# Two transformer blocks on one core: a tenth k-pair per half of the down projections by seven products, with the stationary sums in a ring of nine places

## The reference, cut to what matters

```
x = x + (gelu(u_gate) * u_val) @ w_ffn_down        # block 1: [256, 5632] @ [5632, 2048]
x = x + (silu(gate) * up) @ w_ffn_down_2           # block 2: the same shapes
```

## Time and profile before

| | us |
|---|---|
| median of three runs | 2571.33 |
| the profiled execution, its own time | 2572.12 |
| its span, from the first to the last instruction | 2570.2 |
| PE busy (share of the span) | 2559.9 (100%) |
| DVE busy | 1693.3 (66%) |
| ACT busy | 1346.9 (52%) |
| SP, raw weights of the down projections: 88 loads of 1024 KB | 4.9 each from issue to landing (median) |

### The profile page before, as it was taken

One profiled execution on the slowest core, in us unless ns is written; L12 is line 12 of the kernel. 1 busy time (PEld: TensorE's weight loads), 2 busy tenths in 40 slices (PEclk: granted clock), 3 DMA queues, 4 the chain that ended last, 5 costly groups with the idle time before them and its releaser, 6 DMA issues.

```text
span 2570.2 us, 34530 instructions
## 1 busy us (share of the span) xinstructions
PE 2559.9 (100%) x12410; PEld 2131.0 (83%) x12410; DVE 1693.3 (66%) x2069; ACT 1346.9 (52%) x1729; POOL 99.6 (4%) x110
## 2 busy tenths in 40 slices
PE   9999999999999999999999999999999999999998
PEld 8887788888888888888887888888888888888887
DVE  6656556877777788875667565465555554547888
ACT  5455545666555554555645466434544444445454
POOL 2000000111111100000000000000000000000000
PEclk9999999999999999999999999999999999999999
DMA  7745555666665575655555545555566665657564
GB/s 242 220 149 156 165 188 172 215 206 206 189 188 190 167 284 196 225 184 187 186 172 156 164 154 158 194 190 183 177 209 198 215 197 187 193 186 255 203 216 161
DMA packets 281419, 493.82 MB, mean 192 GB/s; under 512 B 14578, under 2 KB 123236, under 8 KB 281056
## 3 DMA queue, kind: packets, MB, share of 16 engines
q1 hardware_dynamic: 277952, 478.73, 57.3%
q0 software_dynamic: 3184, 13.41, 1.6%
q10 hardware_dynamic: 176, 0.27, 0.1%
HBM read 483.17 MB, written 9.18 MB: 192 GB/s over the span
## 4 chain that ended last, share of the span: by engine, by line
PE 98%; DVE 1%; ACT 0%; issue 0%; DVEq 0%; ACTq 0%
PE acc L771 19%; PE acc L773 19%; PE acc L772 19%; PE acc L1071 13%; PE acc L1064 7%; PE tp L1115 3%; PE tp L1117 3%; PE tp L1116 3%; PE acc L1115 3%; PE acc L1117 3%; PE acc L1116 3%; PE tp L799 1%; PE tp L862 1%; PE tp L844 1%; PE tp L854 0%; PE tp L908 0%
## 5 line engine op out<-in xcount | busy, mean ns | idle before, releaser
L1941 DVE TENSOR_TENSOR WL<-WR,WH 128x1024 fp32r<-128x1024 f32 x712 | 882.7, 1241 | 704.6 <-ACT WH L1392 703.4
L1392 ACT ACTIVATE WH<-WR 128x1024 fp32r<-128x1024 f32 x712 | 754.0, 1059 | 878.1 <-PE acc L773 717.3
L771 PE MATMUL acc<-WH,A 128*128 128x512 f32 x1328 | 523.7, 394 | 0.4 <-DVE A L2009 0.3
L773 PE MATMUL acc<-WH,A 128*128 128x512 f32 x1328 | 517.5, 390 | 0.0
L772 PE MATMUL acc<-WL,A 128*128 128x512 f32 x1328 | 517.1, 389 | 0.0
L1071 PE MATMUL acc<-A,WH 128*128 128x512 f32 x1408 | 336.4, 391 | 0.0
L1071 PEld LDWEIGHTS acc<-A,WH 128*128 128x128 f32 x1408 | 258.6, 188 | 50.0
L771 PEld LDWEIGHTS acc<-WH,A 128*128 128x128 f32 x1328 | 249.4, 188 | 54.1 <-issue 4.0
L773 PEld LDWEIGHTS acc<-WH,A 128*128 128x128 f32 x1328 | 249.3, 188 | 53.0
L772 PEld LDWEIGHTS acc<-WL,A 128*128 128x128 f32 x1328 | 249.6, 188 | 49.7
L771 PE MATMUL acc<-WH,XH 128*128 128x512 f32 x544 | 216.4, 398 | 0.0
(11 more groups left out here) (387 smaller groups left out, 3100.5 us busy)
## 6 DMA issues: line engine op xcount, KB each, us to landing
WR<-in_w_in_dram SPq DMA_DIRECT2D x199, 512.0 KB, 3.6
WR<-in_w_ffn_up_dram SPq DMA_DIRECT2D x176, 512.0 KB, 3.6
RAW<-in_w_ffn_down_dram SPq DMA_DIRECT2D x88, 1024.0 KB, 4.9
WR<-in_w_ffn_in_dram SPq DMA_DIRECT2D x176, 512.0 KB, 3.4
WR<-in_w_out_dram SPq DMA_DIRECT2D x64, 512.0 KB, 3.5
WR<-in_w_in_dram SPq DMA_DIRECT2D x65, 256.0 KB, 3.0
WR<-in_w_ple_gate_dram SPq DMA_DIRECT2D x32, 512.0 KB, 4.3
WR<-in_w_branch_a_dram SPq DMA_DIRECT2D x16, 512.0 KB, 3.7
```

Of the source, the lines that this page charges most:

```text
L771: pe.matmul(o, H[:, kt + k, cols], WH[:, s, k], start=begin, stop=False)
L773: mm = pe.matmul(o, L[:, kt + k, cols], WH[:, s, k], start=False, stop=end)
L1392: act.activation(WH[:, n % RING], WR[:, n % RING], ACT.Copy).then_inc(hi_done, 1)
L1941: dve.tensor_tensor(WL[:, n % RING], WR[:, n % RING], WH[:, n % RING].bitcast(F32), ALU.subtract).then_inc(lo_done, 1)
```

## The change

It makes ten instead of nine k-pairs of each half sevens, with new strings for the order, and keeps `STA` at nine places: place k modulo 9 for the k-th seven of a stage (of which there are now 20). The first nine loads stand at steps 2 to 10 of the stage, as before; each further one stands behind the raw weights of the step that is seven steps ahead of its seven, and SP waits for `q_used` of the seven that had the place before. In halves 1 and 3, where the sums of the first half were used again before, the sums are loaded anew. Four semaphores are taken in turn for the loads, so SP also waits there for the load four before. PE now waits for the sums at every seven. During the up projections a tenth set of sums is made and stored.

```diff
-SUM_J = 9
+SUM_J, STA_SLOTS = 10, 9
 PER_HALF = FKT // 2
-EARLY, LATE = "8878787878787878787888", "8887878787878787878788"
+EARLY, LATE = "8878787877878778787888", "8887878787787877878788"
...
-SUM_GROUPS = (range(0, 1), range(1, 2), range(2, 5), range(5, SUM_J))
+SUM_SEMS = 4
+SEVENS = [[q for q in stage if q.seven] for stage in (QUADS1, QUADS2)]
...
-        STA = sb("STA", [P, SUM_J, 2, 3 * P], F32R, at=stationary)
+        STA = sb("STA", [P, STA_SLOTS, 2, 3 * P], F32R, at=stationary)
...
         def sums_landed(q):
-            n = [q.j in group for group in SUM_GROUPS].index(True)
-            return sum_in[n], 16 * len(SUM_GROUPS[n]) * (q.half // 2 + 1)
+            k = (SEVENS[0] + SEVENS[1]).index(q)
+            return sum_in[k % SUM_SEMS], 16 * (k // SUM_SEMS + 1)
+
+        def sums_slot(q):
+            return SEVENS[q.half // 2].index(q) % STA_SLOTS
...
             def load_sums(q):
-                sp.dma_start(STA[:, q.j].rearrange("p h n -> p (h n)").bitcast(F32), sums_out[q.half // 2][q.j]
-                             ).then_inc(sums_landed(q)[0], 16)
+                k = SEVENS[q.half // 2].index(q)
+                landed, count = sums_landed(q)
+                if k >= STA_SLOTS:
+                    sp.wait_ge(q_used, multiplied_by(SEVENS[q.half // 2][k - STA_SLOTS].n))
+                if count > 16:
+                    sp.wait_ge(landed, count - 16)
+                sp.dma_start(STA[:, sums_slot(q)].rearrange("p h n -> p (h n)").bitcast(F32), sums_out[q.half // 2][q.j]
+                             ).then_inc(landed, 16)
+
+            def sums_beside(q):
+                for k, s in enumerate(SEVENS[q.half // 2]):
+                    behind = k + 2 if k < STA_SLOTS else s.n % (2 * PER_HALF) - 7
+                    if behind == q.n % (2 * PER_HALF):
+                        load_sums(s)
...
                 load_raw(w_down, q)
-                if 2 <= q.n < SUM_J + 2:
-                    load_sums([s for s in QUADS1 if s.seven][q.n - 2])
+                sums_beside(q)
...
             def seven(q):
...
                 pe.wait_ge(q_lo, q.split + 1)
-                if q.half % 2 == 0:
-                    pe.wait_ge(*sums_landed(q))
+                pe.wait_ge(*sums_landed(q))
+                at = sums_slot(q)
```

More of the change, by code:

```diff
@@ L334, in two_blocks_kernel @@
         TRR = sb("TRR", [P, 2, 7 * P], F32R, at=o3 + 10240)
-        STA = sb("STA", [P, SUM_J, 2, 3 * P], F32R, at=stationary)
-        junk2 = sb("junk2", [P, NT], at=stationary + SUM_J * 6 * P * 4)
+        STA = sb("STA", [P, STA_SLOTS, 2, 3 * P], F32R, at=stationary)
+        junk2 = sb("junk2", [P, NT], at=stationary + STA_SLOTS * 6 * P * 4)
         ring = stationary + 32768
@@ L341, in two_blocks_kernel @@
                 sb("RAW22", [P, 2, 2 * NT], at=o3)]
-        merge2 = sb("merge2", [P, NT], at=stationary + SUM_J * 6 * P * 4 + 2048)
+        merge2 = sb("merge2", [P, NT], at=stationary + STA_SLOTS * 6 * P * 4 + 2048)
         SPL1 = sb("SPL1", [P, SLOTS, 2, NT], F32R, at=ring + 4096)
@@ L461, in two_blocks_kernel @@
         raw_in = [sem(f"raw_in{n}") for n in range(ENTRIES)]
-        sum_in = [sem(f"sum_in{n}") for n in range(len(SUM_GROUPS))]
+        sum_in = [sem(f"sum_in{n}") for n in range(SUM_SEMS)]
         q_hi, q_sum, q_lo, q_used = sem("q_hi"), sem("q_sum"), sem("q_lo"), sem("q_used")
@@ L647, in _ @@
                     sp.wait_ge(chunk_used, C_DOWN2)
-                if 2 <= n < SUM_J + 2:
-                    load_sums([s for s in QUADS2 if s.seven][n - 2])
+                sums_beside(q)
             for ready, cols in ((scaled_act, slice(0, 2 * NT)), (scaled_dve, slice(2 * NT, D))):
@@ L750, in _ @@
             pool.wait_ge(hb_lo, 2 * (FF // NT))
-            pool.wait_ge(q_used, multiplied_by(QUADS2[PER_HALF + 5].n))
+            pool.wait_ge(q_used, multiplied_by([q.n for q in QUADS2 if q.j == SUM_J + 3][-1]))
             pool.dma_start(fw2[:], final_g2.partition_broadcast(P)).then_inc(sk_fg_in, 16)
@@ L1121, in raw_block, with sum_block @@
                 return block(o, BH[:, kt, cols], BL[:, kt, cols], split, slot, begin, end)
-            def sum_block(o, split, j, m, slot, begin, end):
+            def sum_block(o, split, at, m, slot, begin, end):
                 cols = slice((m - 2) * P, (m - 1) * P)
-                return block(o, STA[:, j, 0, cols], STA[:, j, 1, cols], split, slot, begin, end)
+                return block(o, STA[:, at, 0, cols], STA[:, at, 1, cols], split, slot, begin, end)
             def eight(q, between=None):
@@ L1143, in seven @@
                 pe.wait_ge(q_lo, q.split + 1)
-                if q.half % 2 == 0:
-                    pe.wait_ge(*sums_landed(q))
+                pe.wait_ge(*sums_landed(q))
+                at = sums_slot(q)
                 raw_block(p1, split, 2 * j, 0, s, q.opens, q.ends).then_inc(q_used, 1)
-                sum_block(sums[0][0], split, j, 4, s + 1, False, False).then_inc(q_used, 1)
+                sum_block(sums[0][0], split, at, 4, s + 1, False, False).then_inc(q_used, 1)
                 raw_block(sums[0][1], split, 2 * j + 1, 0, s + 2, False, False).then_inc(q_used, 1)
@@ L1150, in seven @@
                 raw_block(q5, split, 2 * j, 1, t, q.opens, q.ends).then_inc(q_used, 1)
-                sum_block(p7, split, j, 3, t + 1, q.opens, q.ends).then_inc(q_used, 1)
+                sum_block(p7, split, at, 3, t + 1, q.opens, q.ends).then_inc(q_used, 1)
                 pe.wait_ge(q_lo, q.split + 3)
-                sum_block(p6, split, j, 2, t + 2, q.opens, q.ends).then_inc(q_used, 1)
+                sum_block(p6, split, at, 2, t + 2, q.opens, q.ends).then_inc(q_used, 1)
                 mm = raw_block(sums[1][1], split, 2 * j + 1, 1, t + 3, False, False)
```

## The result

| | us |
|---|---|
| before, median of 6 runs (2571.16 to 2573.11) | 2571.45 |
| after, median of 6 runs (2589.61 to 2592.81) | 2592.05 |
| ratio, 95% interval | 1.0078 [1.0065, 1.0091] |
| forecast (range) | 2588.8 (2584 to 2593) |
| profiled execution of after, its span | 2592.73, 2591.0 |

The change makes the kernel 20.6 us slower, and 3.2 us slower than forecast. The page of the kernel after, against the earlier trace rows: span; busy us and instructions by engine; the chain that ended last.

The account below looks back on a forecast made before the run. The prediction took PE's matmul queue as the bound. Waits and late eights at sevens in a row 18.9, restarts 1.1, norm weight 0.2, less 2.7 for removed matmuls, gave +17.5 us: 2588.8 us, range 2584 to 2593.

Parts of the forecast that it names:

- The bound and the mechanism: Down stages: PE's matmul queue sets the time; DVE, held by 11 places, may never run more than a step ahead.
- Two sevens in a row, 2.05 and 2.73 us: Second seven waits for places still in use: PE stands 2.05 us at six pairs, 2.73 us at two.
- late eight: The eight behind each of the two 2.73 us pairs comes 0.57 us late.
- Restarts: PE is not at full pace at once after a wait: 0.10 us, for eleven late starts 1.1 us.
- Norm weight: Half 3: the norm weight at step 11 stands before the eight of step 12; some 0.2 us come through.
- Costed at nothing: Tenth set of sums, POOL's extra store, PE's and SP's new waits, and the extra loads: no time added.
- Rival C: The extra loads delay the raw weights: up to 6 us more, 2589 to 2595 us; chance 5%.
- granted clock 1.00 in both stages, else B: Sign for the profile after: the granted clock stays at 1.00 through both down stages, otherwise B holds.
- B: Clock falls in the eight waits, each slowing the next step by about 5 us: some 2629 us; chance 3%.
- Rival A: Down stages: DVE's average decides, its lead carries over two sevens in a row, PE stands nowhere: 2568.6 us; chance 5%.
- Idle time that it has over a half can't be saved up: Down stages: DVE, never more than a step ahead, cannot use its idle time over a half as lead.
- A's condition of 14 places: For DVE's average to decide, two sevens in a row need 14 places, and there are 11.

Follow-up runs that it names:

- The order alone: The kernel before, still nine sevens a half and its own loads, but reordered so two sevens stand in a row twice a half: 2592.79 us.
- fifteen places: The changed kernel with 15 instead of 11 places for split weights, and four instead of nine places for the sums: 2567.25 us.
- The ring: The changed kernel with nine sevens a half in the old order, sums still in nine places and loaded anew: 2571.53 us, ratio 1.0001.
- the filled kernel: The changed kernel with eight more matmuls on PE between two sevens in a row, altering part of the result: 2586.91 us.
- fourteen places: The changed kernel with 14 instead of 11 places for split weights, and four instead of nine for the sums: 2584.43 us.
- the kernel with fifteen places and the norm weights moved: The kernel with fifteen places, with the norm weights of half 3 behind steps 15 and 17 instead of 11 and 13: 2566.38 us.
- the doubles alone: The same run as The order alone: 2592.79 us, ratio 1.0081 against the kernel before.
- thirteen places: The changed kernel with 13 instead of 11 places for split weights, and four instead of nine for the sums: 2590.72 us.
- one double: The changed kernel with another order in stage 2 alone, two sevens in a row once a half instead of twice: 2588.86 us.
- the remainders first: The changed kernel, but in a seven DVE makes the first group's remainders before the sums instead of behind them: 2588.06 us.

## Why the prediction was right, and where not

- *The bound and the mechanism: right.* PE's queue sets the time, DVE may not run ahead further than the places allow, and two sevens in a row take that lead. The places walked step by step gave the kind of each of the eight waits and their positions. The order alone reproduces the loss (2592.8 us), and fifteen places remove it (2567.3).
- *Two sevens in a row, 2.05 and 2.73 us: measured 1.94 and 2.62.* Release to DVE 0.10 us (0.12 forecast), DVE 4.35 (4.34), DVE to PE 0.05 (0.15). The last comes from the earlier trace rows, where it may already hold something else; it is most of the 0.1 us a wait. One late eight of 0.45 us instead of two of 0.57; the second was covered by a clock fall, as said above. In sum 17.4 instead of 18.9 us.
- *Restarts: 0.9 instead of 1.1 us. Norm weight: 0 instead of 0.2.* No wait of PE stands at step 12 of half 3. It can show where the double has no other slack: 0.87 us with fifteen places.
- *Costed at nothing: right.* The ring, 18 of the 22 loads and the waits for them gave a ratio of 1.0001, known to a thousandth. Rival C is out. All between the stages, the up projection of block 2 included, takes the same 1200.28 us with the tenth set of sums.
- *The step that failed: "granted clock 1.00 in both stages, else B".* B was weighed as all or nothing, each wait bringing 5 us, and given 3%. The clock did fall, behind three of eight waits, and for eight matmuls each, some 1.6 us a time: 4.8 us that the sum had not. The prediction's range held the time because this missing term and the terms that came out too large (1.5 + 0.2 + 0.2 us, and 1.0 us of small waits that became less) partly cancel. That is luck: with 4.8 us more and nothing else changed the forecast would be 2593.6 us, above its own range. The Trainium skill (TensorE: Matmul & The Clock Gate, section HAM oscillation — how this bites in real kernels) tells of a clock that falls in every wait of a loop, where the waits are for a DMA and longer than any here. By it waits as short as these would bring no fall; the measurement decides otherwise. Behind waits of 1.94 to 2.62 us the clock fell in three of eight cases, and the filled kernel shows that the waits were the cause.
- *Rival A, DVE's average decides: refuted for eleven, thirteen and fourteen places; with fifteen PE stands at one double only, and the time (2567.3 us) is near A's 2568.6.* "Idle time that it has over a half can't be saved up" does not hold with fifteen places. A's condition of 14 places was wrong.

What stays open: what picks the three waits of eight. The changed kernel's falls lie behind waits of both kinds, and equal waits 28 us apart in the same half differ.

## What to carry to other kernels

Where a producer runs ahead through a ring of buffers, its share of busy time says nothing on whether two heavy steps in a row fit: walk the places, with the group sizes and the end of the ring, and see when the last group of each of the two steps comes free. Count in the order before the amount, since moving sevens together cost 21 us, while the tenth seven takes 2.7 us of matmuls away (the kernel with fifteen places and the norm weights moved gained 5.1 us in all). And a wait of TensorE can have a second price, the slow matmuls behind it; it goes away with filler work as well as with the wait, which makes it measurable apart.

## What the runs showed of the hardware

- *The clock falls behind short waits, but not always.* Over the changed kernel and the runs with the doubles alone, thirteen places, fourteen places and one double, 35 times PE's starts in a down stage lay 2.1 to 2.9 us apart for a wait on DVE at a double; behind 14 of them 7 or 8 starts at 0.40 to 0.45 us followed. In the same kernels and with the remainders first there are 23 gaps of 0.8 to 1.8 us between starts in the down stages, and behind none of them did such a start follow. No half of any kernel had more than one fall.
- *It begins at once or up to 1.6 us later.* In the changed kernel the first six starts behind the wait are at 0.23 to 0.34 us and the half pace begins 1.5 us behind the wait's end (959.34 against 957.84); with the doubles alone, 0.7 us behind it (956.88 against 956.22). In two of the 14 falls it begins with the first start (2512.19 in the changed kernel, 1095.64 with fourteen places).
- *The first matmul behind a wait at a double takes 0.33 or 0.34 us to the next start* instead of 0.2267 (where the half clock begins at once, 0.45 and 0.41 us), with the filled waits too (956.28 to 956.62), where PE had been busy with other matmuls until then.
- *The column of the granted clock can miss a slow stretch.* At the start of the profiled execution after it stands at 1.00 while the starts are 0.43 us apart (8.23, 8.65, 9.08, 9.51, 9.93), nine matmuls in 3 us; before they were 0.23 us apart there. 0.43 us is the pace of the half clock; that it was the clock there too isn't shown:

```profile
8.00:11.00 3.00, 3.00 (x9) 2.33 (x9) 2.73 (x5) 2.75 (x5) 1.89 (x4) 1.00 1.06 402
```

So read the distance of two starts beside the column.
